# Last layer norm: columns 512 to 767 of the second token half scaled on GpSimd, the others kept in PSUM

## The reference

```
def layer_norm(x, g, b, eps=1e-5):
    mu = xf.mean(-1)
    var = jnp.square(xf - mu).mean(-1)
    return (xf - mu) * lax.rsqrt(var + eps) * g + b

for i in range(2):
    m = mixer(h)                                   # layer 0: sparse and stick-breaking, layer 1: MoBA
    h = layer_norm(DEEPNORM_ALPHA * h + m, ln_mix_g[i], ln_mix_b[i])
    f = swiglu(h, ffn_gate[i], ffn_up[i], ffn_down[i])
    h = layer_norm(DEEPNORM_ALPHA * h + f, ln_ffn_g[i], ln_ffn_b[i])
```

## Time and profile before

| | us |
|---|---|
| median of 3 runs | 598.95 (598.15 to 599.94) |
| profiled execution, its own time | 598.9 |
| its span in the profile | 597.1 |
| busy: PE, DVE, ACT, POOL | 589.6, 424.2, 342.3, 26.7 |
| DMA | 109.43 MB, mean 183 GB/s |

### The profile page before, as it was taken

How to read it: one execution, slowest core, us unless ns; L and a number is a source line. 1 busy time by engine, 2 the same in 40 slices (tenths; PEclk the granted TensorE clock), 3 DMA queues, 4 the chain that set the end, 5 groups by cost and what they waited for, 6 DMA issues and landing times.

```text
span 597.1 us, 9595 instructions
## 1 busy us (share of the span) xinstructions
PE 589.6 (99%) x3354; PEld 506.7 (85%) x3354; DVE 424.2 (71%) x697; ACT 342.3 (57%) x645; POOL 26.7 (4%) x49
## 2 busy tenths in 40 slices
PE   9999999999999999999999999999999999999995
PEld 7988888888888888888888888888888888888885
DVE  4699877886776556655887888768677666665637
ACT  5767986456655544554556767645565455555430
POOL 1111111100000000000010000002000000000000
PEclk9999999999999999999999999999999999999999
DMA  8756437286676555564447543662767665556401
GB/s 314 254 180 200 142 116 249 95 288 205 217 230 203 196 197 183 184 208 140 143 141 275 182 140 114 208 212 75 237 219 241 208 192 180 182 178 190 140 1 70
DMA packets 30113, 109.43 MB, mean 183 GB/s; under 512 B 3377, under 2 KB 3377, under 8 KB 29953
## 3 DMA queue, kind: packets, MB, share of 16 engines
q1 hardware_dynamic: 28368, 102.25, 51.6%
q0 software_dynamic: 1568, 6.23, 3.3%
q10 hardware_dynamic: 144, 0.52, 0.2%
HBM read 107.94 MB, written 1.05 MB: 183 GB/s over the span
## 4 chain that ended last, share of the span: by engine, by line
PE 99%; DVE 0%; DVEq 0%; issue 0%; ACT 0%; POOL 0%; ACTq 0%; POOLq 0%
PE bank L1244 27%; PE bank L1152 24%; PE bank L1158 13%; PE bank L1694 5%; PE bank L1522 3%; PE bank L1698 3%; PE bank L1145 2%; PE bank L1222 2%; PE bank L1197 2%; PE bank L1198 2%; PE bank L1204 2%; PE bank L1339 1%; PE bank L1350 1%; PE bank L1330 1%; PE bank L1526 1%; PE bank L1501 1%
## 5 line engine op out<-in xcount | busy, mean ns | idle before, releaser
L753 DVE TENSOR_TENSOR wboth<-raw,wboth 128x1024 fp32r<-128x1024 f32 x190 | 225.1, 1223 | 45.4 <-ACT wboth L376 44.5
L376 ACT CAST wboth<-raw 128x1024 fp32r<-128x1024 f32 x190 | 191.3, 1047 | 22.1 <-DMA raw<-stream_in 20.9
L1152 PE MATMUL bank<-hTs,wboth 128*128 128x512 f32 x640 | 152.2, 390 | 0.0
L1244 PE MATMUL bank<-wboth,oThi 128*128 128x512 f32 x468 | 150.1, 392 | 0.0
L1152 PEld LDWEIGHTS bank<-hTs,wboth 128*128 128x128 f32 x640 | 118.8, 188 | 23.7
L1244 PEld LDWEIGHTS bank<-wboth,oThi 128*128 128x128 f32 x468 | 88.0, 188 | 18.3 <-issue 0.7
L1244 PE MATMUL bank<-wboth,oTlo 128*128 128x512 f32 x234 | 91.3, 390 | 0.0
L1158 PEld LDWEIGHTS bank<-hTs,wboth 128*128 128x128 f32 x640 | 81.9, 191 | 3.0
L1158 PE MATMUL bank<-hTs,wboth 128*128 128x256 f32 x640 | 83.2, 283 | 0.0
L1244 PEld LDWEIGHTS bank<-wboth,oTlo 128*128 128x128 f32 x234 | 44.0, 188 | 8.1
L654 ACT COPY kT<-bank 128x256 f32<-128x256 f32 x40 | 14.8, 371 | 59.0 <-PE bank L1158 59.0
(11 more groups left out here) (189 smaller groups left out, 637.2 us busy)
## 6 DMA issues: line engine op xcount, KB each, us to landing
raw<-stream_in SPq DMA_DIRECT2D x190, 512.0 KB, 4.8
qT<-ln_rows_in POOLq DMA_DIRECT2D x8, 512.0 KB, 5.1
kT<-stream_in SPq DMA_DIRECT2D x2, 512.0 KB, 6.0
h<-x_in POOLq DMA_DIRECT2D x1, 1024.0 KB, 5.0
out<-h SPq DMA_DIRECT2D x4, 256.0 KB, 2.1
v<-xT_in ACTq DMA_DIRECT2D x1, 512.0 KB, 5.0
v<-xT_in SPq DMA_DIRECT2D x1, 512.0 KB, 6.5
dist<-consts_in POOLq DMA_DIRECT2D x1, 384.0 KB, 3.6
```

What stands on the lines that cost most here:

```text
L376: nc.scalar.copy(whi[:, c % RING, j * HW:(j + 1) * HW], raw[:, c % RAW, j * HW:(j + 1) * HW]).then_inc(whi_ready, 1)
L753: nc.vector.tensor_tensor(wlo[:, c % RING, cols], raw[:, c % RAW, cols], whi[:, c % RING, cols].bitcast(F32), ALU.subtract).then_inc(wlo_r ...
L1152: mm(dst[:], whi[:, slot, off + k * P:off + (k + 1) * P], hTs[:, k].rearrange("p j s -> p (j s)"), start=(k == 0), stop=False)
L1244: last = mm(bank[4 + 2 * t + a][:], o[:, kts[j], t * P:(t + 1) * P], w[:, c % RING, j * D + a * 512:j * D + (a + 1) * 512], start=(start a ...
```

## The change

Before, for the second token half of the last norm, DVE wrote `ALPHA * h + bank` to `h` in SBUF for columns 0 to 767, scaled all 1024 columns in two instructions and finished them in two. After it:

- columns 0 to 511 stay in bank 6: line 827 writes there, the statistics read there, line 848 scales them there in place, and line 859 writes to `h`;
- columns 768 to 1023 stay in bank 2 through line 848 too, and the second instruction of line 859 covers these 256 columns alone;
- columns 512 to 767 go to `h` in SBUF as before, but from there POOL does all: it waits for `mv` and `rstd`, then `(x - mean) * rstd`, then `* g`, then `+ b`, three instructions of 128 x 256, each waiting for the one in front;
- SP's last store waits for POOL as well as for DVE.

```diff
+        third_moved, third_scaled, third_done = sem("third_moved"), sem("third_scaled"), sem("third_done")
...
                     sp.wait_ge(norm_ready, 12 + 2 * t + a + 1)
+                    if t and a:
+                        sp.wait_ge(third_done, 1)
                     sp.dma_start(out[t][:, cols], h[:, t, cols]).then_inc(stored, 16)
...
+            third = h[:, 1, 2 * S:3 * S]
+            pool.wait_ge(rows_loaded, 128)
+            pool.wait_ge(mv_ready, 8)
+            pool.wait_ge(rstd_ready, 8)
+            nc.gpsimd.tensor_scalar(third, third, mv[:, 1, 0:1], rstd[:, 1:2], ALU.subtract, ALU.mult
+                                    ).then_inc(third_moved, 1)
+            pool.wait_ge(third_moved, 1)
+            nc.gpsimd.tensor_tensor(third, third, grow[:, 2 * S:3 * S], ALU.mult).then_inc(third_scaled, 1)
+            pool.wait_ge(third_scaled, 1)
+            nc.gpsimd.tensor_tensor(third, third, brow[:, 2 * S:3 * S], ALU.add).then_inc(third_done, 1)
...
                         if t and a and last:
                             hh = hh[:, 0:S]
-                        nc.vector.scalar_tensor_tensor(out=hh, in0=hh, scalar=ALPHA,
-                                                       in1=bank[4 + 2 * t + a][:, 0:hh.shape[1]],
+                        acc = bank[4 + 2 * t + a][:, 0:hh.shape[1]]
+                        res = acc if last and t and a == 0 else hh
+                        nc.vector.scalar_tensor_tensor(out=res, in0=hh, scalar=ALPHA, in1=acc,
                                                        op0=ALU.mult, op1=ALU.add).then_inc(res_done, 1)
                         dve.wait_ge(res_done, 2 * k + a + 1)
-                        nc.vector.bn_stats(stats[:, t, 6 * a:6 * a + 6], hh).then_inc(stat_done, 1)
+                        nc.vector.bn_stats(stats[:, t, 6 * a:6 * a + 6], res).then_inc(stat_done, 1)
...
                     if last and t:
-                        for at, src in ((slice(0, 3 * S), h[:, 1, 0:3 * S]), (slice(3 * S, 4 * S), quarter)):
-                            nc.vector.scalar_tensor_tensor(out=h[:, 1, at], in0=src, scalar=mv[:, 1, 0:1],
+                        for at, src, dst in ((slice(0, 2 * S), bank[6][:], bank[6][:]),
+                                             (slice(3 * S, 4 * S), quarter, quarter)):
+                            nc.vector.scalar_tensor_tensor(out=dst, in0=src, scalar=mv[:, 1, 0:1],
                                                            in1=grow[:, at], op0=ALU.subtract, op1=ALU.mult
                                                            ).then_inc(scaled, 1)
...
                         dve.wait_ge(scaled, 2 * k + a + 1)
-                        nc.vector.scalar_tensor_tensor(out=h[:, t, cols], in0=h[:, t, cols],
+                        if last and t:
+                            src = quarter if a else bank[6][:]
+                            if a:
+                                cols = slice(3 * S, 4 * S)
+                        else:
+                            src = h[:, t, cols]
+                        nc.vector.scalar_tensor_tensor(out=h[:, t, cols], in0=src,
                                                        scalar=rstd[:, t:t + 1], in1=brow[:, cols], op0=ALU.mult,
                                                        op1=ALU.add).then_inc(norm_ready, 1)
```

## The result

The kernel after takes 599.58 us (median of 19 runs, 599.34 to 600.95), the one before 598.63 (19 runs, 598.15 to 599.96). The ratio is 1.0016, with a 95% interval of 1.0009 to 1.0022: slower by 0.95 us, and the interval puts it between 0.5 and 1.3. That is half of the 0.3% that the prediction took for what can be told, but with 19 runs of each it is clear of the noise.

A forecast was written before the change was run, and what follows sets the result against it. PE bounds the kernel until 591.1 us, then the tail; POOL's chain, 592.50 + 0.41 + 0.09 + 0.74 + 0.09 + 0.74 = 594.57, sets the last store 0.04 earlier, giving 598.9 us. Range 598.1 to 600.2.

The forecast's parts named there:

- 0.04 us earlier: Last store's issue: 594.60 instead of 594.64, making the median 598.91, rounded 598.9; this case within 0.2 had chance 0.48.
- DVE's part: Scaling and finishing after the aggregation: last instruction ends at 594.07 instead of 594.62, 0.55 shorter for the second store.
- POOL's start: POOL's first instruction in the tail starts 0.09 us after rstd is known at 592.41, so at 592.50.
- The first operation: POOL's `(x - mean) * rstd` on 128x256: 0.41 us, priced by a one-input mask, with 0.74 as upper bound.
- The two waits of POOL for itself: Between POOL's three instructions: 0.09 us each, with bounds of 0.03 and 0.25.
- The two operations with two tensors: POOL's `* g` and `+ b`, inputs in SBUF: 0.74 us each, from twelve instances between 728 and 747 ns.
- SP behind POOL: SP issues the last store 0.03 us after POOL ends at 594.57, so at 594.60.
- the time around the span: Execution time outside the profiled span: 1.8 us around 597.1, taken over unchanged.
- it waited for nothing: Second store before the change: data began at 595.51, issue plus 0.85 is 595.49, so no delay from the first store.
- Rival 1: POOL's chain is longer, first operation 0.74 and each wait 0.25: 0.61 us more, 599.55; chance 0.34.
- Rival 2: In the tail DVE and POOL shut each other out: 1.62 us more than before, 600.6; chance 0.06.
- The cap by the stores: Last two stores' data moves back to back, so at most 0.26 us is gained of DVE's 0.55.

The follow-up runs named there:

- e4_psum_only: Kernel after with POOL idle: DVE scales columns 512 to 767 in a third instruction and finishes in two of 512; 598.71 against 598.54 before, ratio 1.0002.
- e8_one_wait: Kernel after without POOL's wait for the mean's semaphore; ran once, no time given, POOL started 0.19 behind rstd in place of 0.22.
- e1_bench: Kernel after plus six POOL operations, run eight times each where POOL would idle, last norm unchanged; single time 599.67 us.
- e7_cheap_first: Kernel after with POOL's first operation replaced by subtracting the repeated mean alone, all waits kept; 599.04 against 598.57 before, ratio 1.0007.
- e2_quiet: Kernel after with DVE's four scaling and finishing instructions of the last token half waiting for POOL's first operation; single time 600.92 us.
- e9_no_third: Kernel after without POOL's three instructions and the wait for them, columns 512 to 767 stored unnormalised; 598.25 against 598.50 before, ratio 0.9996.
- e5_bcast: Kernel after, POOL only subtracts the repeated mean without awaiting rstd and multiplies by g, DVE finishes the rest; 598.46 against 598.57 before, ratio 0.9997.

## Why the prediction was wrong

The range held the time, and the time lay within 0.3%, but the forecast was "0.04 us earlier" and it came 0.95 later, clear of the noise. The forecast stood on a median of three runs, 598.95, that lies 0.32 above that of 19, so 598.9 looks nearer to 599.58 than the sum was. Step by step, counted from the aggregation up to the issue of the last store:

- DVE's part: forecast 2.22, measured 2.23. Right. That data in PSUM costs DVE nothing was right as well (e4_psum_only).
- POOL's start: forecast 0.09 behind rstd, measured 0.22, so 0.13 missed. It was priced by a start behind ACT in the earlier trace rows; e8_one_wait shows that the extra wait isn't it. What it is stays open.
- **The first operation, the step that failed:** "I take 0.41, because it reads one tensor". It took 1.22, 0.81 more, and lay beyond the upper bound of 0.74 too. Both ends were rows of other operations: a mask and a two-tensor multiply. The number of tensors read isn't what sets this operation's price: in e1_bench every form with one tensor took longer than the multiply of two.
- The two waits of POOL for itself: forecast 0.09 each, measured 0.09 and 0.08. Right.
- The two operations with two tensors: forecast 0.74, measured 0.72. Right, 0.04 in all.
- SP behind POOL: forecast 0.03, measured 0.08.

The sum of the misses is 0.13 + 0.81 - 0.01 - 0.04 + 0.05 = 0.94, and -0.04 + 0.94 = 0.90, the measured shift of the last store. The mechanism was right, that POOL's chain sets the end and DVE's relief is worth nothing behind it; one term was sized a third of what it is. A second term was put at nothing without a reason: the time around the span, taken over as 1.8, was 1.95 in the kernel after and 1.74 in the one before, 0.2 us. The landing went 0.07 the other way; "it waited for nothing", said of the second store before, is not quite so, as alone it lands 0.07 sooner. Cheapening only the first operation (e7_cheap_first) brought the last store 0.67 us forward, which is what shows that the loss sits there.

Rival 1 was this case in kind, but its 0.61 fell short of 0.90, and it put part of it on the waits, which took 0.09 and 0.08 and not 0.25. That its 599.55 is the measured 599.58 is luck: its loss was too small by 0.3 and its base too high by as much.

The Trainium skill, GPSIMD Engine Reference, section 3.1, gives 1.03 cycles an element to such a body, from which the prediction had an estimate of 0.22 us for the loop of the first operation, and section 4.1 calls one-input operations roughly line-rate. The runs don't agree: they show 3.3 ns a column and 0.37 us once, and a one-input form at 925 ns longer than a two-input one at 740. Here the measurement decides. Rival 2, the shutting out, is refuted for this tail by e2_quiet, where the first operation takes 1.22 us alone as well, and by DVE's finishing instructions, 0.74 beside POOL and 0.74 in e4_psum_only without it. The Trainium skill, SBUF — State Buffer, Who interferes with whom, says that a DVE instruction with at most one SBUF input doesn't contend with GpSimd, and the traces agree: each of DVE's instructions there reads one tensor from PSUM and one from SBUF.

The cap by the stores was right: e9_no_third gained 0.3 in landing of 0.54 in issue. So even a POOL that cost nothing would have brought 0.3 us, and e5_bcast shows that the 0.25 around the span can take most of that back.

## What to carry to other kernels

When work moves to an engine that has never run that very operation in the trace, a row of another operation of the same shape is no bound for it (here the upper bound of 0.74 stood against 1.22); put the operation in an idle stretch and read its duration first. Before relieving an engine in a tail, work out which chain ends next and what it may cost at most: here 2.2 us lay between rstd and the old end of DVE, and POOL's three steps took 3.05 from rstd on, with their waits. A step that needs only the mean shouldn't wait for rstd: e5_bcast puts it there and fits. And when a gain is read from a trace, the time less the span belongs beside it, for both kernels.

## What the runs showed that I had not expected

- On POOL, subtracting a per-partition value takes 925 ns over 256 columns as the scalar form, and 614 ns as a two-input operation whose second input is that value repeated.
- The scalar form with two operations and two pointers grows by 3.3 ns a column between 128 and 256 columns, which leaves 0.37 us paid once; the pointers are 0.14 of its 1.22 us.
- A 128 KB store lands 2.0 us after its issue, as a 256 KB one does when nothing is in front of it; two of 256 KB issued 0.39 us apart make the second take 2.3.
- Three short instructions at the end of POOL's stream went with 0.2 us more outside the span, where no row of the timeline stands, and with one instruction packet behind its end.
